# A gated linear recurrence before a mixture of experts: key products on VectorE, 128-column level products, and the heads overlapped

## The reference, cut to what matters

```python
f = lb + (1 - lb) * sigmoid(f_logit); logf = log(f); k = 1 - f; q = silu(q)
b = cumsum(logf)                        # inside a chunk
inter = (q * exp(b)) @ state            # what earlier chunks left
att[t, s] = sum_k q[t,k] * exp(b[t,k] - b[s,k]) * k[s,k]    # s <= t
out = inter + att @ v
state = exp(b_last) * state + (k * exp(b_last - b)).T @ v
```

## Time and profile before

| | |
|---|---|
| Median of 3 runs | 2455.72 us (2454.97 to 2459.82) |
| The profiled execution | 2460.58 us, of it span 2459.0 us |
| PE busy | 2213.6 us (90%) |
| DVE busy | 1597.7 us (65%) |
| ACT busy | 1352.4 us (55%) |
| POOL busy | 474.6 us (19%) |
| Mean granted clock | 0.938 |
| The recurrence in the trace | from 426.75 us (first `args`) to 597.55 us (last matmul seen by the waiting queues) |

### The profile page before, as it was taken

How to read it: one execution, slowest core, us unless ns; L and a number is a source line. 1 busy time by engine, 2 the same in 40 slices (tenths; PEclk the granted TensorE clock), 3 DMA queues, 4 the chain that set the end, 5 groups by cost and what they waited for, 6 DMA issues and landing times. The chain is left out here.

```text
span 2459.0 us, 38622 instructions
## 1 busy us (share of the span) xinstructions
PE 2213.6 (90%) x10494; PEld 1838.7 (75%) x10495; DVE 1597.7 (65%) x2261; ACT 1352.4 (55%) x2036; POOL 474.6 (19%) x478
## 2 busy tenths in 40 slices
PE   5999886876993999999999999999999999999992
PEld 4888775876783787877877878777877878778781
DVE  4121167775554777767777676778778677776874
ACT  5211245333231766767666576667667576675764
POOL 3000000321023112113121131213121131121320
PEclk9999978666995999999999999999999999999996
DMA  5111100000333879889798897989798797987976
GB/s 175 39 43 52 69 18 10 9 9 28 117 102 133 280 221 321 263 264 307 226 318 262 263 308 223 318 266 348 233 307 280 245 322 232 303 282 236 326 236 238
DMA packets 260585, 506.15 MB, mean 206 GB/s; under 512 B 34281, under 2 KB 35306, under 8 KB 260368
## 3 DMA queue, kind: packets, MB, share of 16 engines
q1 hardware_dynamic: 241874, 456.02, 55.1%
q0 software_dynamic: 18656, 49.45, 8.6%
q10 hardware_dynamic: 4, 0.02, 0.0%
HBM read 466.24 MB, written 39.17 MB: 206 GB/s over the span
## 5 line engine op out<-in xcount | busy, mean ns | idle before, releaser
L1611 DVE TENSOR_TENSOR wlo<-raw,whi 128x1024 fp32r<-128x1024 f32 x774 | 927.4, 1217 | 110.6 <-ACT whi L1110 92.3
L1110 ACT ACTIVATE whi<-raw 128x1024 fp32r<-128x1024 f32 x775 | 807.0, 1057 | 220.5 <-PE ps L881 125.6
L551 PE MATMUL ps<-whi,xTh 128*128 128x512 f32 x1024 | 405.7, 396 | 0.0
L552 PE MATMUL ps<-wlo,xTh 128*128 128x512 f32 x1024 | 400.8, 391 | 0.0
L553 PE MATMUL ps<-whi,xTl 128*128 128x512 f32 x1024 | 400.5, 391 | 0.0
L1851 POOL DMA_INDIRECT acc_d<-y,icur x64 | 114.3, 1786 | 1031.8 <-ACT y L1152 1022.1
L551 PE MATMUL ps<-whi,aTh 128*128 128x512 f32 x512 | 214.7, 419 | 24.1 <-DVE aTl L1655 24.1
L553 PEld LDWEIGHTS ps<-whi,xTl 128*128 128x128 f32 x1024 | 192.8, 188 | 41.3
L552 PEld LDWEIGHTS ps<-wlo,xTh 128*128 128x128 f32 x1024 | 193.1, 189 | 40.0
L551 PEld LDWEIGHTS ps<-whi,xTh 128*128 128x128 f32 x1024 | 193.1, 189 | 38.7
L553 PE MATMUL ps<-whi,aTl 128*128 128x512 f32 x512 | 202.0, 394 | 0.0
(11 more groups left out here) (285 smaller groups left out, 3983.7 us busy)
## 6 DMA issues: line engine op xcount, KB each, us to landing
raw<-in_w SPq DMA_DIRECT2D x776, 512.0 KB, 6.9
raw<-in_w_in SPq DMA_DIRECT2D x16, 512.0 KB, 3.7
xs<-in_x SPq DMA_DIRECT2D x8, 512.0 KB, 6.1
raw<-in_w_out SPq DMA_DIRECT2D x8, 512.0 KB, 3.7
mix<-in_x SPq DMA_DIRECT2D x8, 512.0 KB, 4.1
acc_d<-mix SPq DMA_DIRECT2D x8, 512.0 KB
h_d<-h SPq DMA_DIRECT2D x8, 512.0 KB
mix<-acc_d SPq DMA_DIRECT2D x8, 512.0 KB, 6.6
```

The lines of the kernel that those rows point to most:

```text
L551: pe.matmul(o, sh, mh_, start=start, stop=False, skip_group_check=skip)
L552: pe.matmul(o, sh, ml_, start=False, stop=False, skip_group_check=skip)
L1110: act.activation(slot(whis, s), slot(raws, s), ACT.Copy).then_inc(split_hi, 1)
L1611: dve.tensor_tensor(slot(wlos, s), slot(raws, s), slot(whis, s).bitcast(F32), ALU.subtract).then_inc(split_lo, 1)
```

## The change

- **Key products.** POOL has no product any more. DVE does them at each level behind the query product (128 x 512), and at L = 7 as one 128 x 1024 product. `prod_pool` is gone.
- **L = 7.** DVE's subtraction is gone. ACT forms `exp(b_last - b)` straight from `hf` by scale -1 and a bias column, in 8 instructions of 128 x 128.
- **Wide levels.** A level's matmul takes all 128 columns of `hp` as moving side; a level fills two banks (0, 1 or 2, 3, by L's parity). The copy reads the upper-half columns out of them, with a stride.
- **Places.** `q * exp(b)` gets its own buffer `hpx` (in the place of `reset` and `g2row`); the output goes to banks 4, 5, the diagonal to 6, 7, the states' increments to 2, 3.
- **Order on PE.** The next head's diagonal and its level 0 stand ahead of a head's outputs. `used_by` gives the counts of `level_used` in this order. `outs` stands one step later on ACT, and so do the squares.
- **SP.** The load of `g2row` stands behind the last `rec_out`, ahead of `rw`.

```diff
-            return (LEVELS + 1) * (s // STEPS) + min(s % STEPS, LEVELS) + 1
+            return LEVELS * (s // STEPS) + s % STEPS + 1
+        def used_by(s):
+            hd, L = divmod(s, STEPS)
+            if L == 0 and hd > 0:
+                return s
+            if L == LEVELS + 1 and hd < HH - 1:
+                return s + 2
+            return s + 1
...
-            sp.dma_start(g2row[:, :], norm2_g.broadcast_to([P, D])).then_inc(late_in, 16)
             sp.dma_start(rb[:, :], router_b.broadcast_to([P, NE])).then_inc(late_in, 16)
...
             sp.wait_ge(rec_out, 2 * HH)
+            sp.dma_start(g2row[:, :], norm2_g.broadcast_to([P, D])).then_inc(late_in, 16)
...
+            def diagonal(hd):
-                    pe.wait_ge(rec_out, 2 * hd)
+                    pe.wait_ge(level_copied, LEVELS * (hd - 1) + 1)
-                    m = pe.matmul(ps[:, 2 + t // 4, (t % 4) * P:(t % 4 + 1) * P],
+                    m = pe.matmul(ps[:, 6 + t // 4, (t % 4) * P:(t % 4 + 1) * P],
...
+            def level(hd, L):
+                pe.wait_ge(prod_dve, dve_prods_by(s))
+                if L >= 2:
+                    pe.wait_ge(level_copied, lev - 1)
+                elif hd > 0 and L == 0:
+                    pe.wait_ge(level_copied, lev)
+                elif hd > 0:
+                    pe.wait_ge(states_set, hd)
-                        m = pe.matmul(ps[:, lev % 2, t * 64:(t + 1) * 64], v,
-                                      v.rearrange("p (m two h) -> p m two h", two=2, h=h)[:, :, 1, :],
+                    m = pe.matmul(ps[:, 2 * (L % 2) + t // 4, (t % 4) * P:(t % 4 + 1) * P], v, v,
+                                  start=True, stop=True)
...
+            diagonal(0)
+            level(0, 0)
+            for hd in range(HH):
+                if hd > 0:
+                    outputs(hd - 1)
+                for L in range(1, LEVELS):
+                    level(hd, L)
+                states(hd)
+                if hd + 1 < HH:
+                    diagonal(hd + 1)
+                    level(hd + 1, 0)
+            outputs(HH - 1)
...
+                elif L == LEVELS:
+                    act.wait_ge(prod_dve, dve_prods_by(s - 2))
+                    for t in range(NT):
+                        m = act.activation(he[:, s % 2, t * P:(t + 1) * P], hf[:, hd, t * P:(t + 1) * P], ACT.Exp,
+                                           scale=-1.0, bias=hf[:, hd, t * P + P - 1:t * P + P])
+                    m.then_inc(exp_set, 1)
...
-                if L == 1 and hd > 0:
+                if L == 2 and hd > 0:
                     outs(hd - 1)
...
-                elif L == LEVELS:
-                    bv, ev = (z.rearrange("p (t n) -> p t n", n=P) for z in (b, e))
-                    dve.tensor_tensor(ev, bv[:, :, P - 1:P].broadcast_to([P, NT, P]), bv, ALU.subtract).then_inc(arg_set, 1)
...
+                    dve.tensor_tensor(ov, qv, ev, ALU.mult)
+                    ov, kv, ev = (z.rearrange("p (m two h) -> p m two h", two=2, h=h)[:, :, 0, :]
+                                  for z in (hp[:, s % 2, :], hk[:, hd, :], he[:, s % 2, :]))
+                    dve.tensor_tensor(ov, kv, ev, ALU.mult).then_inc(prod_dve, 1)
+                elif L == LEVELS:
+                    dve.tensor_tensor(hp[:, s % 2, :], hk[:, hd, :], he[:, s % 2, :], ALU.mult).then_inc(prod_dve, 1)
...
-                        ps[:, lev % 2, :].rearrange("p (t m h) -> p t m h", t=NT, h=h)))
+                        ps[:, 2 * (L % 2):2 * (L % 2) + 2, :].rearrange(
+                            "p a (t m two h) -> p (a t) m two h", t=4, two=2, h=h)[:, :, :, 1, :]))
...
-                    pool.tensor_tensor(o, k, e, ALU.mult).then_inc(prod_pool, 1)
-                elif L == LEVELS:
-                    pool.tensor_tensor(hp[:, s % 2, :], hk[:, hd, :], he[:, s % 2, :], ALU.mult).then_inc(prod_pool, 1)
```

More of the change, by code:

```diff
@@ L123, in build @@
     reset = at("reset", A + 52 * KB, [P, T])
+    hpx = at("hpx", A + 52 * KB, [P, T])
     attT = [at("attT0", A + 48 * KB, [P, NT, P]), at("attT1", A + 56 * KB, [P, NT, P])]
@@ L682, in _, with states @@
                 m.then_inc(diag_done, 1)
[L683 to L692, removed]
-                        m = pe.matmul(ps[:, lev % 2, t * 64:(t + 1) * 64], v,
-                                      v.rearrange("p (m two h) -> p m two h", two=2, h=h)[:, :, 1, :],
-                                      start=True, stop=True)
-                    m.then_inc(level_used, 1)
+            def level(hd, L):
+                s = STEPS * hd + L
+                lev = LEVELS * hd + L
+                pe.wait_ge(prod_dve, dve_prods_by(s))
[6 more added lines that the diff above has]
+                for t in range(NT):
+                    v = hp[:, s % 2, t * P:(t + 1) * P]
+                    m = pe.matmul(ps[:, 2 * (L % 2) + t // 4, (t % 4) * P:(t % 4 + 1) * P], v, v,
+                                  start=True, stop=True)
+                m.then_inc(level_used, 1)
+            def states(hd):
                 s = STEPS * hd + LEVELS
-                pe.wait_ge(prod_pool, pool_prods_by(s))
+                pe.wait_ge(prod_dve, dve_prods_by(s))
                 if hd > 0:
-                    pe.wait_ge(kbT_set, 2 * hd)
+                    pe.wait_ge(rec_out, 2 * hd)
                 for t in range(NT):
@@ L706, in _, with outputs @@
                 pe.wait_ge(kbT_set, 2 * hd + 2)
-                if hd > 0:
-                    pe.wait_ge(states_set, hd)
+                pe.wait_ge(level_copied, LEVELS * hd + 6)
                 for t in range(NT - 1):
-                    m = pe.matmul(ps[:, 6 + t // 4, (t % 4) * P:(t % 4 + 1) * P], kbT[:, t, :],
+                    m = pe.matmul(ps[:, 2 + t // 4, (t % 4) * P:(t % 4 + 1) * P], kbT[:, t, :],
                                   hv[:, t, hd * P:(hd + 1) * P], start=True, stop=True)
                 m.then_inc(added_state, 1)
+            def outputs(hd):
                 s = STEPS * hd + LEVELS + 1
@@ L722, in _ @@
                     if t > 0:
-                        m = pe.matmul(o, hp[:, s % 2, t * P:(t + 1) * P], state[:, t - 1, :],
+                        m = pe.matmul(o, hpx[:, t * P:(t + 1) * P], state[:, t - 1, :],
                                       start=False, stop=True)
                 m.then_inc(level_used, 1)
+            diagonal(0)
[10 more added lines that the diff above has]
+            outputs(HH - 1)
             pe.wait_ge(rec_out, 2 * HH)
@@ L1043, in _ @@
                                        ACT.Copy).then_inc(kbT_set, 1)
-                if L == 1 and hd > 0:
+                if L == 2 and hd > 0:
                     outs(hd - 1)
                     act.wait_ge(rec_out, 2 * hd)
-                if 2 <= L < 6 and hd > 0:
-                    for t in range(2 * L - 4, 2 * L - 2):
+                if 3 <= L < 7 and hd > 0:
+                    for t in range(2 * L - 6, 2 * L - 4):
                         square(t, hd, junks[:, :])
@@ L1407, in prods @@
                 dve.wait_ge(exp_set, s + 1)
-                if s >= 2:
-                    dve.wait_ge(level_used, s - 1)
+                was = s - (STEPS if L == LEVELS + 1 else 4 if L == 1 else 2)
+                if was >= 0:
+                    dve.wait_ge(level_used, used_by(was))
                 if L < LEVELS:
```

49 lines of the change are left out of this document (17 added, 32 removed).

## The result

The changed kernel takes 2416.55 us in the median of 4 runs (2414.92 to 2420.0), against 2456.92 us (2454.97 to 2459.82): 40 us less, a ratio of 0.9837 with an interval of 0.982 to 0.9854. In a second comparison on another chip it was 2418.09 against 2456.62 us, ratio 0.9845 (0.9828 to 0.9862). The forecast was 2421 us, with a chance of 0.91 for faster.

The account below looks back on a forecast made before the run. The prediction took the 170.8 us recurrence, with VectorE and TensorE waiting for each other, as the bound. Its terms, -6.9 + 5.6 - 34.1 + 1 - 3.2 + 3 = -34.6 us, gave 2421 us, range 2409 to 2440.

Parts of the forecast that it names:

- Waits for products, outputs and diagonal, -34.1: VectorE's recurrence waits would go: 13.1 us for level products, 13.6 for outputs, 7.4 for the diagonal.
- Key products, L = 7 and stretches, -6.9: On VectorE: 21.4 us of key products added; 9.1 of L = 7 subtractions, 14.2 and 5.0 of stretches removed.
- New wait of L = 7, +5.6: At each head's last key product, VectorE would wait 1.4 us for ScalarE's exponentials, over four heads.
- Outs +1, start and small gaps +3: New waits around ScalarE's outs +1 us; head 0 before the clock rises +1, semaphores +2.
- Tail -3.2: Last head at the high clock: state increments 1.5 us shorter, outputs 1.7 us shorter.
- Wide levels cost nothing, strided reads cost nothing: In levels: doubled columns add 0 to 0.04 us each; the copy's strided PSUM read adds 0, at most 20 us overall.
- rival 3: Strided PSUM reads slow VectorE's 28 level copies; from 1.95 us each the gain is gone, 2464 us at 2.25; chance 0.03.
- SP, 0: Loading g2row and rw behind the last rec_out costs 0; without the cover up to 3.3 us.
- One sign of being wrong: In the changed profile, level copies taking over 1 us would show the prediction wrong; it expected 0.71 us.
- the clock coming and going: Rival 1: half of the levels and head borders run at the low clock; +12 us, 2433 us; chance 0.21.
- rival 2: TensorE's clock stays low throughout the recurrence: 168 us against 170.8, kernel 2453 us; chance 0.06.
- Rival 4: GpSimd did not cause VectorE's stretch, so -6.9 becomes +12.3 us and the kernel takes 2440 us; chance 0.03.

Follow-up runs that it names:

- order: Changed kernel with TensorE's old order: diagonal, levels, states and outputs of a head before the next head's diagonal; recurrence 149.6 us, kernel 2434.67 us.
- buffer: Changed kernel with q * exp(b) back in the shared product buffer instead of its own; recurrence 140.2 us, kernel 2424.66 us.
- narrow kernel: Changed kernel with level matmuls taking only the 64 upper-half columns again (also called width); recurrence 145.3 us, kernel 2430.74 us.
- the copy that writes in one run: Changed kernel with copies of levels 5 and 6 writing 64 columns per chunk in one run, leaving these levels out; recurrence 132.1 us, total not read.
- the idle work: Changed kernel plus 28 GpSimd products on buffers nobody else uses, one after each level's exponential; recurrence 142.7 us, kernel 2430.67 us.
- order, banks, buffer and L = 7: Changed kernel with narrow level matmuls and key products back on GpSimd, both at once; recurrence 148.5 us, kernel 2432.01 us.

## Why the prediction was right

The mechanism was the one forecast: waits go, VectorE's own work sets the pace, the clock rises with wide products (in head 0, from 0.50 between 425 and 430 us to 1.00 from 435 us on) and then stays up inside the levels. The size was 34.6 us by the sum and 37.9 us in the recurrence, but that they lie so close is partly luck, since misses cancel. By its terms:

- **Waits for products, outputs and diagonal, -34.1.** Measured -32.8 on VectorE (34.2 before, 1.4 after). Right. That the parts carry it is shown by the undone edits: order +16.7, buffer +7.3, width +12.4.
- **Key products, L = 7 and stretches, -6.9.** VectorE's busy time fell by 2.6 us. The term that failed is the copy's stretch: I took 24.9 - 28 x 0.71 = 5.0 us as GpSimd's doing. Without it the term is -1.9. The copy's 0.71 was that of level 4 alone, and I wrote that the write side "has the same stride in all rows and costs nothing". The copies of levels 5 and 6 take 1.3 us in every kernel here that writes them to their places, before and after, by their write pattern; this is shown by the kernel with narrow levels and the kernel before with its keys on VectorE (means of 884 and 881 ns without GpSimd) and by the copy that writes in one run. The trace of before already had it. Its copy of level 5 stood beside GpSimd's large product, but that of level 6 began when the product had ended, and was as long:

```profile
452.70 1.31 DVE L1434 COPY_PREDICATED attT<-maskL,ps 128x512 f32<-128x512 int32 x1
453.25 2.36 POOL L1787 TENSOR_TENSOR hp<-hk,he 128x1024 f32<-128x1024 f32 x1 [2.25 <-ACT he L1032]
...
456.55 1.29 DVE L1434 COPY_PREDICATED attT<-maskL,ps 128x512 f32<-128x512 int32 x1 [2.54 <-PE ps L693]
```

  The rows to read would have been all copies of one head in turn, not a mean against one row. The first subtraction's stretch, 14.2 us by my account, was GpSimd's: its group fell by 13.9 us (33.3 to 19.4).
- **New wait of L = 7, +5.6.** Measured 3.0, of which the profile puts 2.0 to TensorE's level 5, in whose buffer it writes, and 0.8 to ScalarE, against 0.9 before: +2.1. The 8 exponentials took 2.45 us, as priced; the list ahead of the wait was longer than I had counted, with a copy of 1.3.
- **Outs +1, start and small gaps +3.** Not there. The idle time before the first subtraction fell from 6.5 to 3.7 us instead; 1.2 us of that were waits for GpSimd's product, and the gap behind each copy is 0.15 us now and was 0.21.
- **Tail -3.2.** The increments gave -1.8 (3.3 to 1.5), the outputs nothing: after 2.8 us of waiting they began at the low clock, as before, and took 5.25 us both times.
- **Wide levels cost nothing, strided reads cost nothing.** Right: 1.86 us at the full clock, and no change of the copy's time between reading in runs and with a step. That also rules out rival 3.
- **SP, 0.** Right.

The misses add up to the 3.3 us between 34.6 and 37.9: too much gain by 1.3 (waits), 4.3 (work) and 1.4 (tail), too much cost by 3.5 (L = 7) and 6.8 (the +4 of the two terms behind it, which came out as -2.8). One sign of being wrong that the prediction names did come, copies of over 1 us: eight of the 28, but they had been as long before, so they took nothing from the gain.

Of the rivals, the clock coming and going did happen, near the borders of heads and not within the levels. The prediction had it at 1.00 from the second head on. It cost little, because VectorE was busy for 4.6 us or more of these 5 us windows:

```profile
480.00:485.00 5.00, 3.83 (x22) 3.59 (x21) 4.71 (x8) 2.35 (x4) 0.00 (x0) 0.70 0.02 3
510.00:515.00 5.00, 2.45 (x14) 2.22 (x15) 4.76 (x6) 2.67 (x4) 0.00 (x0) 0.77 0.00 2
515.00:520.00 5.00, 5.00 (x28) 5.00 (x27) 4.64 (x12) 1.13 (x2) 0.00 (x0) 0.55 0.00 0
```

A low clock throughout was not run. The narrow kernel comes nearest, at 0.50 inside its levels and up to 1.00 at the borders, and costs 12.4 us of the 32 us that rival 2 had over the forecast. Rival 4 (GpSimd not the cause of the stretch) is ruled out for the subtraction by the idle work and by the kernel before with its keys on VectorE (692 ns); for the copy it was right.

As parts of the 37.9 us: order, banks, buffer and L = 7 give 22.3, and on top of them keys and width together 15.6, of which 3.2 and 5.9 come singly and 6.5 only jointly.

## What to carry to other kernels

When two engines wait for each other in turns, count one engine's own work per round and the waits by releaser: their sum gave this change to within 10%, though partly because misses cancelled. Keys and width were worth more together (15.6 us) than singly (3.2 and 5.9), so a part that shows nothing by itself, as the key move on the kernel before, is not yet shown to be worthless. An edit whose profile gains or loses 1.5 us may owe it to the clock of the last products alone; look at their window before reading it. Before a long duration is put down to a neighbour, look whether the same operation with the same pattern is long elsewhere, without that neighbour. A wait for an instruction's own landing belongs ahead of the next instruction that needs it, and not behind the one that posts it.

## What the runs showed of the hardware

- In the levels of the narrow kernel (fp32 products of 64 moving columns) the granted clock was 0.50 with TensorE busy 5.00 of 5 us; in the same window of the changed kernel (128 moving columns) it was 1.00 with TensorE busy 2.54 of 5 us. 16 instructions took 3.49 us at the low clock in both forms (level and diagonal of the kernel before) and 1.83 to 1.86 us at the high one. Doubling the columns shortened the recurrence by 12.4 us.
- A predicated copy on VectorE (512 elements per partition, fp32) took 0.70 to 0.75 us where it writes runs of 4 or more elements and 1.3 us with runs of 2 or 1; the query product of the same levels, with the same steps, took 0.69 us. Reading every second run of PSUM instead of one run added nothing (884 ns both).
- A GpSimd product on buffers of its own (1.28 us) stretched VectorE's first subtraction, both of whose operands lie in SBUF, from 0.69 to 1.07 us in the level shown and to 1.00 us in the mean of 28. It left the copy from PSUM alone (0.71 us beside it), and the copy did not stretch it.
- Standing still behind the landing of each copy cost VectorE 0.27 us a level (a round of 3.28 us against 3.01), 0.15 us of it idle time and the rest lost overlap. Moving 28 such waits to the next copy shortened the recurrence by 6.1 and 4.5 us.
